# The step widths loaded as a small tile ahead of the weight stream, and the first norm's root, sums and splits in another order

## The chip, the cores and the metric

The kernel runs on one core of one Trainium2 chip. The metric is the device time of one execution in microseconds (us), from three runs. A core has five engines that run side by side and meet through semaphores: TensorE (PE, matrix products; PEld is its weight load), VectorE (DVE), ScalarE (ACT), GpSimd (POOL) and SyncE (SP), which here only issues DMAs.

## The reference

Two transformer-like layers over a sequence of 256 tokens of width 1024, all in float32. What matters here is how the first one begins:

```python
h = rmsnorm(x, mix_pre_norm[l])        # x * rsqrt(mean(x*x) + 1e-6) * w
u = h @ w_in[l]
u_z, u_xbc, u_dt, u_ly, u_lx, u_g = jnp.split(u, list(IN_SPLITS), axis=-1)
...
dt = jax.nn.softplus(u_dt + dt_bias)   # u_dt: 16 columns, one for each head of the SSD mixer
xbc = jax.nn.silu(causal_dwconv(u_xbc, conv_w, conv_b))
```

`u_dt` are the step widths: 16 of the input projection's columns. The rest of the kernel (two mixers, gates, a feed-forward part, then a second layer with four branches) is the same in both versions.

## The kernel before, in words

Activations lie with features on the 128 partitions and tokens along the free axis: `X` is 8 tiles of 128x256. Every weight passes through one **stream**: `stream_list` names its chunks in order, most of them 256 output columns, that is two **units** of 128x1024 floats (512 KB). The stream has 260 units. SP fetches unit q into one of `NR` = 5 buffers `RAW` (`t_raw`), and for q of 5 and more it waits until unit q-5 has been split. Splitting keeps float32 accuracy with three fast products: ACT copies the unit to a rounded high part `WH` (`split` on ACT, L1232), DVE subtracts to get the low part `WL` (`split` on DVE, L1739; its event is `lo(q)`), both in one of `NS` = 4 buffers, and PE does `three` for each of 8 tiles k (L605, L606, L607): wh by xh, wh by xl, wl by xh. A unit is so 24 matmuls of 128x256.

Each engine's program is written out in one order. The class `Walk` keeps it in step: `walk.unit(ahead)` takes the next unit q and first issues the splits up to q+ahead (3 unless told otherwise), `walk.cols(name)` does so for each unit of a chunk with a `tick` behind each, and a tick lets the lanes (generators with the side work) go on if their time has come. So what an engine does between two splits delays the later one.

The start goes like this. The chunk `dt` is the first of the stream, one unit (q=0): its 128 columns hold the 16 step widths, and the rest of its product is not used. `xbc4`, `xbc5` follow (q=1 to 4), then `g0` (q=5, 6), `xbc0` (7, 8), `g1` (9, 10), `xbc1` (11, 12). `dt`, `xbc4` and `xbc5` are computed from x times the norm's weight (`YBh`, `YBl` in `t_br`) without the root, and scaled by the token's factor afterwards (`ROWR`), since the norm is not known yet. Beside that ACT squares x into `SC0` (8 tiles), DVE adds some of the squares (`square_adds`), PE sums over partitions by products with a column of ones (`norm_sums_first`, `norm_sums_last`, `column_sums`), DVE makes the reciprocal root for 2 columns with an integer guess and three Newton steps (`rsqrt`, `newton`), and PE spreads it over the partitions (`norm_spread`). `h_parts` on DVE (L1754 into `t_arena`, L1744 into `t_hl`), ACT (L1237 into `t_hh`) and POOL (L2448, the odd tiles of `t_hl`) then make the normed input `Hh`, `Hl`, which `g0` is the first chunk to use; `chunk_by_k` there takes both units tile by tile. `norm_spread` stands behind `xbc4` on PE; `h_parts` stands behind all of `xbc5` on DVE and ACT.

Behind `g0`, DVE scales `xbc4` by `ROWR` (L1744, 128x512) and does the convolution's six taps (`xbc_taps`, L1754), for which ACT first evacuates `g0` (`gates(0)`, a tanh; it waits for `hb`, three small operations of DVE, too) and does `conv_first`. Between and behind these come the splits, and the softplus of the step widths.

## Time and profile before

| | |
|---|---|
| median of 3 runs | 880.71 us (880.54 to 880.88) |
| the profiled execution | 881.82 us, its span 880.0 us |
| mean granted clock of TensorE | 0.995 |
| busy share | PE 98%, PEld 89%, DVE 71%, ACT 58%, POOL 8% |
| read from memory | 147.18 MB, 168 GB/s over the span |

The span runs from the first to the last instruction; the profiled execution's own time is 1.82 us longer than its span and 1.11 us above the median. Busy shares are means over stages with different limits.

### The profile page before, as it was taken

The numbers are of one execution on the slowest core, as the hardware profiler recorded it, in microseconds if no ns is written. First come the engines' busy times: TensorE is split into PE (matmuls) and PEld (weight loads), VectorE is DVE, ScalarE is ACT, GpSimd is POOL, SyncE is SP. The second block draws the span as 40 slices with busy tenths as digits, with TensorE's granted clock in tenths as the row PEclk, the third lists the DMA queues.
The fourth block names the chain that finished last, engine by engine and source line by source line (L and its number), as shares of the span: only waits on it lengthen the run. The fifth ranks groups of instructions, "written<-read, shape, count | busy, mean of one in ns | idle before, by whom it ended". The sixth has DMA issues, their size and how long they took to land.

```text
span 880.0 us, 14646 instructions
## 1 busy us (share of the span) xinstructions
PE 859.8 (98%) x5816; PEld 780.8 (89%) x5816; DVE 623.1 (71%) x1124; ACT 509.1 (58%) x826; POOL 73.6 (8%) x76
## 2 busy tenths in 40 slices
PE   6999999999999999999999999999999999999997
PEld 6999999999989999999998799999999776778885
DVE  6787987988867766666656787787456455775765
ACT  5565777665377656656657688544444434454443
POOL 0200002001020211111113000500000000000000
PEclk9999999999999999999999999999999999999999
DMA  9457443457455655555564555643322322365541
GB/s 344 146 194 276 159 145 108 169 179 291 140 186 174 239 190 175 187 191 175 185 198 137 181 188 201 222 145 124 117 97 96 113 104 96 119 205 195 197 146 48
DMA packets 40588, 149.21 MB, mean 170 GB/s; under 512 B 4524, under 2 KB 4680, under 8 KB 39880
## 3 DMA queue, kind: packets, MB, share of 16 engines
q1 hardware_dynamic: 40520, 148.27, 49.3%
q8 instruction: 46, 0.75, 0.3%
q14 instruction: 22, 0.18, 0.1%
HBM read 147.18 MB, written 1.08 MB: 168 GB/s over the span
## 4 chain that ended last, share of the span: by engine, by line
PE 89%; DVE 5%; ACT 3%; issue 1%; DMA 1%; SPq 0%; DVEq 0%; ACTq 0%
PE bank L610 40%; PE bank L605 16%; PE bank L606 16%; PE bank L607 16%; PE bank L613 2%; DVE t_wl L1739 2%; DVE t_arena L1744 1%; DVE t_arena L1754 1%; DVE t_x L1754 1%; ACT t_hh L1237 1%; DMA t_x<-in_xin 1%; DVE t_sm L1751 1%; ACT t_arena L1237 1%; ACT t_wh L1232 0%; ACT t_br L1237 0%
## 5 line engine op out<-in xcount | busy, mean ns | idle before, releaser
L1739 DVE TENSOR_TENSOR t_wl<-t_raw,t_wh 128x1024 fp32r<-128x1024 f32 x260 | 316.5, 1226 | 114.3 <-ACT t_wh L1232 113.4
L1232 ACT ACTIVATE t_wh<-t_raw 128x1024 fp32r<-128x1024 f32 x260 | 273.4, 1058 | 129.1 <-PE bank L610 60.3
L605 PE MATMUL bank<-t_hh,t_wh 128*128 128x256 f32 x1144 | 330.3, 289 | 2.2 <-DVE t_hl L1744 1.5
L607 PE MATMUL bank<-t_hh,t_wl 128*128 128x256 f32 x1144 | 323.6, 283 | 0.0
L606 PE MATMUL bank<-t_hl,t_wh 128*128 128x256 f32 x1144 | 323.5, 283 | 0.0
L605 PEld LDWEIGHTS bank<-t_hh,t_wh 128*128 128x128 f32 x1144 | 219.1, 192 | 6.1 <-issue 4.2
L606 PEld LDWEIGHTS bank<-t_hl,t_wh 128*128 128x128 f32 x1144 | 219.2, 192 | 0.8
L607 PEld LDWEIGHTS bank<-t_hh,t_wl 128*128 128x128 f32 x1144 | 219.1, 192 | 0.0
L610 PE MATMUL bank<-t_wh,t_br 128*128 128x512 f32 x384 | 123.8, 393 | 0.2 <-POOL t_br L2448 0.2
L1754 DVE SCALAR_TENSOR_TENSOR t_arena<-bank,t_par,t_arena 128x255 f32<-128x255 f32 (+2 forms) x184 | 75.3, 474 | 45.0 <-ACT t_arena L1237 44.7
L610 PE MATMUL bank<-t_wh,t_hh 128*128 128x512 f32 x224 | 92.0, 411 | 1.8 <-DVE t_wl L1739 1.8
L610 PE MATMUL bank<-t_wh,t_hl 128*128 128x512 f32 x224 | 88.3, 394 | 0.0
L610 PE MATMUL bank<-t_wl,t_hh 128*128 128x512 f32 x224 | 88.0, 393 | 0.0
L610 PEld LDWEIGHTS bank<-t_wh,t_br 128*128 128x128 f32 x384 | 72.1, 188 | 16.5 <-issue 1.9
L1237 ACT ACTIVATE t_arena<-bank 128x512 f32<-128x512 f32 (+4 forms) x75 | 42.6, 582 | 69.5 <-PE bank L610 57.8
L610 PE MATMUL bank<-t_wl,t_br 128*128 128x512 f32 x192 | 74.9, 390 | 0.0
L2448 POOL TENSOR_TENSOR t_br<-t_arena,t_br 128x256 fp32r<-128x256 f32 x30 | 34.5, 1153 | 437.4 <-ACT t_br L1237 437.4
L610 PE MATMUL bank<-t_arena 128*128 128x128 f32 (+6 forms) x432 | 66.7, 297 | 0.8 <-DVE t_arena L1744 0.8
L610 PEld LDWEIGHTS bank<-t_arena 128*128 128x128 f32 (+3 forms) x432 | 52.0, 176 | 12.7 <-issue 8.2
L1237 ACT ACTIVATE t_arena<-bank,t_par 128x256 f32<-128x256 f32 x76 | 37.6, 546 | 39.3 <-PE bank L607 39.3
L610 PEld LDWEIGHTS bank<-t_wh,t_hh 128*128 128x128 f32 x224 | 42.4, 189 | 12.8 <-DVE t_wl L1739 3.2
L610 PEld LDWEIGHTS bank<-t_wh,t_hl 128*128 128x128 f32 x224 | 42.3, 189 | 9.4
(152 smaller groups left out, 840.3 us busy)
## 6 DMA issues: line engine op xcount, KB each, us to landing
t_raw<-in_ws SPq DMA_DIRECT2D x260, 512.0 KB, 3.9
t_br<-decay SPq DMA_DIRECT2D x1, 2048.0 KB, 8.3
t_arena<-in_post SPq DMA_DIRECT2D x3, 512.0 KB, 5.5
t_arena<-gates SPq DMA_DIRECT2D x1, 1536.0 KB, 10.5
t_x<-in_xin SPq DMA_DIRECT2D x4, 256.0 KB, 5.5
t_bd<-in_bd SPq DMA_DIRECT2D x1, 1024.0 KB, 11.7
t_x<-in_xtok SPq DMA_DIRECT2D x1, 1024.0 KB, 5.8
t_arena<-in_mem SPq DMA_DIRECT2D x1, 1024.0 KB, 8.0
```

The source lines that it names most:

```text
L605: e.matmul(o, wh, xh, start=first, stop=False, skip_group_check=True)
L606: e.matmul(o, wh, xl, start=False, stop=False, skip_group_check=True)
L607: return e.matmul(o, wl, xh, start=False, stop=last, skip_group_check=True)
L610: return e.matmul(o, l, r, start=st, stop=sp, skip_group_check=True)
L613: return e.transpose(o, i, ident[0:i.shape[0], 0:i.shape[0]])
L1232: e.activation(WH[q % NS][:, :], RAW[q % NR][:, :], ACT.Copy, bias=0.0, scale=1.0).then_inc(*hi.now(q))
L1237: return e.activation(o, i, f, bias=bias, scale=scale)
L1739: e.tensor_tensor(WL[q % NS][:, :], RAW[q % NR][:, :], WH[q % NS][:, :].bitcast(F), SUB).then_inc(*lo.now(q))
L1744: return e.tensor_tensor(o, a, b, op)
L1751: return e.tensor_scalar(o, a, s1, s2, op0, op1)
L1754: return e.scalar_tensor_tensor(out=o, in0=a, scalar=s, in1=b, op0=op0, op1=op1)
L2448: return e.tensor_tensor(o, a, b, op)
```

## The change

- The chunk `dt` leaves the stream, which has 259 units then. The 16 columns of step widths and the norm's weight come as one tile of 128x136, `first`, by the first DMA. ACT and DVE split the 16 columns into `DTS` (high part beside low part, 32 columns), and PE multiplies with 32 and 16 stationary columns: 16 matmuls. Where the two parts meet is a product with `fold`, in place of a transposition.
- The DMA order becomes `first`, the four pieces of x, unit 0, the constants, unit 1, the parameters, and the rest of the units.
- ACT and DVE make `YBh`, `YBl` before they split unit 0.
- PE does five float32 products of a tile of zeros into bank 3 first. Nothing reads them.
- The squares are added up by DVE to one tile (two additions more), the column sums over it stand between the two units of `xbc4`, the root is ACT's square root, a reciprocal on DVE and one Newton step. ACT loads the table of the square root at its start.
- `h_parts` on DVE and ACT moves ahead of the splits of later units: on DVE only the units up to 4 are split before it. `g0` is done by units (`chunk_by_units`).

The diff, cut to its core (a line of "..." stands for lines left out):

```diff
     s = []
-    s.append(("dt", "w_in", rng(DTC, 128)))
...
 CON = [("ident", 128), ("ones", 128), ("strict", 128),
-       ("b16", 128), ("b32", 128), ("b64", 128)]
+       ("b16", 128), ("b32", 128), ("b64", 128), ("fold", 16)]
...
 def bank_table():
-    bank, n = {}, 0
+    bank, n = {}, 1
...
         DTR = ar(84, 4, T)
+        DTW = ar(86, 136)
+        DTX, WMIX = DTW[:, 0:128].rearrange("p (k c) -> p k c", k=8), DTW[:, 128:136]
+        DTS = WH[NS - 1][:, 0:256].rearrange("p (k c) -> p k c", k=8)
...
         cols_dt = SM[:, 96:160].rearrange("p (a b) -> p a b", a=4)
-        dtr, acs = DTR[0:16, 0, :], DTR[0:16, 1, :]
+        dtr, acs = DTR[0:32, 0, :], DTR[0:16, 1, :]
...
                 e.dma_start(RAW[q % NR][:, :], ws[c, :, 1024 * u:1024 * u + 1024]).then_inc(s_raw[q % NR], 16)
-            fetch(0)
-            e.dma_start(parT[:, :], par).then_inc(s_par, 16)
+            e.dma_start(DTW, first).then_inc(s_first, 16)
             for i in range(4):
                 e.dma_start(X[:, 2 * i:2 * i + 2, :], xin[:, 2 * i:2 * i + 2, :]).then_inc(s_x[i], 16)
+            fetch(0)
             e.dma_start(conT[:, :], con).then_inc(s_con, 16)
-            for q in range(1, NR):
+            fetch(1)
+            e.dma_start(parT[:, :], par).then_inc(s_par, 16)
+            for q in range(2, NR):
...
                     e.dma_start(POSTW["fpost"], post[1]).then_inc(s_post["fpost"], 16)
-                if q == 24:
+                if q == 23:
                     e.wait_ge(*d_dt.of("acs"))
                     e.dma_start(decay, acs).then_inc(s_decay[0], 16)
-                if q == 27:
+                if q == 26:
...
                     walk.tick()
+            def chunk_by_units(name, xh, xl, x_ready):
+
+                b = BANK[name]
+                for j in range(2):
+                    q = walk.unit(NS - 1 - j)
+                    wh, wl = weights(q, 8)
+                    split_ready(q)
+                    if j == 0:
+                        bank_free(name)
+                    for k in range(8):
+                        if j == 0:
+                            x_ready(k)
+                        m = three(half(b, j), wh[:, k, :], wl[:, k, :], xh[:, k, :], xl[:, k, :], k == 0, k == 7)
+                    m.then_inc(*unit.now(q))
...
                 return m
+            def mix_sums():
+                e.wait_ge(s_con, 16)
+                e.wait_ge(*d_add.of("mix", 3))
+                column_sums(7, 0, [SC0[:, 0, :]], True, True).then_inc(*p_norm.now("mix", "sum"))
...
                 for hf in range(2):
-                    m = tr(PB[6][:, 16 * hf:16 * hf + 16], dtr[:, 128 * hf:128 * hf + 128])
+                    m = mm(PB[6][:, 16 * hf:16 * hf + 16], dtr[:, 128 * hf:128 * hf + 128], cn("fold", 16)[0:32, :])
...
             walk.lanes = [ssd_lane(), lru_lane(), rows_lane(), dn_lane(), gm_xm_lane(), sw_lane()]
-            chunk_by_k("dt", YBh, YBl, x_weighted)
-            e.wait_ge(s_con, 16)
-            norm_sums_first("mix", 7, SC0)
-            norm_sums_last("mix", 7, SC0)
-            chunk("xbc4", YBh, YBl)
+            e.wait_ge(*d_const.of("warm"))
+            for _ in range(5):
+                mm(PB[3][:, 0:T], SC1[:, 0, 0:128], SC1[:, 0, :])
+            e.wait_ge(*d_dt.of("w"))
+            for k in range(8):
+                e.wait_ge(*d_xw.of(k))
+                mm(PB[6][0:32, 0:T], DTS[:, k, :], YBh[:, k, :], k == 0, False)
+                m = mm(PB[6][0:16, 0:T], DTS[:, k, 0:16], YBl[:, k, :], False, k == 7)
+            m.then_inc(*p_dt.now("dt"))
+            chunk("xbc4", YBh, YBl, {(1, 0): mix_sums})
...
-                    chunk_by_k("g0", Hh, Hl, normed("mix"))
-                    e.wait_ge(*d_f.of("mix", 7))
+                    chunk_by_units("g0", Hh, Hl, normed("mix"))
+                    e.wait_ge(*d_const.of("row"))
...
                 yield from walk.until(2)
-                chunk_done("dt")
-                act(dtr, half(BANK["dt"], 0)[0:16, :], ACT.Copy).then_inc(*a_dt.now("raw"))
+                e.wait_ge(*p_dt.of("dt"))
+                act(dtr, PB[6][0:32, 0:T], ACT.Copy).then_inc(*a_dt.now("raw"))
...
             walk.lanes = [conv_lane(), ssd_lane(), lru_lane(), rows_lane(), dn_lane(), gm_xm_lane(), sw_lane()]
-            split(0)
-            walk.split_to = 1
-            e.wait_ge(s_par, 16)
+            e.wait_ge(*d_const.of("one"))
+            act(SM[:, 392:393], SM[:, 392:393], ACT.Sqrt)
+            e.wait_ge(s_first, 16)
+            act(DTS[:, :, 0:16], DTX, ACT.Copy).then_inc(*a_dt.now("w"))
...
-                act(YBh[:, k, :], X[:, k, :], ACT.Copy, scale=pc("mixpre", k)).then_inc(*a_xw.now(k))
+                act(YBh[:, k, :], X[:, k, :], ACT.Copy, scale=WMIX[:, k:k + 1]).then_inc(*a_xw.now(k))
+            split(0)
             for i in range(4):
                 act(SC0[:, 2 * i:2 * i + 2, :], X[:, 2 * i:2 * i + 2, :], ACT.Square).then_inc(*a_sq.now("mix", i))
-            walk.cols("dt", True)
-            walk.cols("xbc4")
-            walk.cols("xbc5")
+            split(1)
+            walk.split_to = 2
+            walk.unit(2)
+            e.wait_ge(*d_rs.of("mix", "v"))
+            act(NW[:, 2, 0:2], NW[:, 1, 0:2], ACT.Sqrt).then_inc(*a_sq.now("mix", "root"))
+            walk.tick()
+            e.wait_ge(*p_dt.of("dt"))
+            walk.unit(2)
+            walk.tick()
+            e.wait_ge(s_par, 16)
+            walk.unit()
+            walk.tick()
             h_parts("mix", SC1)
+            walk.unit()
+            walk.tick()
...
                     if k < 8:
-                        stt(f[:, k, :], x[:, k, :], pc(w, k), PB[bank][:, 0:T], MUL, MUL).then_inc(*d_f.now(tag, k))
+                        stt(f[:, k, :], x[:, k, :], w[:, k:k + 1], PB[bank][:, 0:T], MUL, MUL).then_inc(*d_f.now(tag, k))
...
             walk.lanes = [ffn_lane(), ssd_lane(), lru_lane(), rows_lane(), dn_lane(), gm_xm_lane(), sw_lane(), dn_out_lane()]
-            split(0)
-            walk.split_to = 1
+            e.memset(SM[:, 392:393], 1.0).then_inc(*d_const.now("one"))
+            e.memset(SC1[:, 0, :], 0.0).then_inc(*d_const.now("warm"))
+            e.wait_ge(*a_dt.of("w"))
+            tt(DTS[:, :, 16:32], DTX, DTS[:, :, 0:16].bitcast(F), SUB).then_inc(*d_dt.now("w"))
             for k in range(8):
                 e.wait_ge(*a_xw.of(k))
-                stt(YBl[:, k, :], X[:, k, :], pc("mixpre", k), YBh[:, k, :].bitcast(F), MUL, SUB).then_inc(*d_xw.now(k))
+                stt(YBl[:, k, :], X[:, k, :], WMIX[:, k:k + 1], YBh[:, k, :].bitcast(F), MUL, SUB).then_inc(*d_xw.now(k))
+            split(0)
             square_adds("mix", SC0)
-            walk.cols("dt", True)
-            rsqrt("mix", NW, 7, 2, 1024, p_norm.of("mix", "sum"))
-            walk.cols("xbc4")
-            e.wait_ge(*p_norm.of("mix", "row"))
+            e.wait_ge(*a_sq.of("mix", 3))
+            e.wait_ge(*d_add.of("mix", 1))
+            tt(SC0[:, 0:2, :], SC0[:, 0:2, :], SC0[:, 6:8, :], ADD).then_inc(*d_add.now("mix", 2))
+            e.wait_ge(*d_add.of("mix", 2))
+            tt(SC0[:, 0, :], SC0[:, 0, :], SC0[:, 1, :], ADD).then_inc(*d_add.now("mix", 3))
+            split(1)
+            walk.split_to = 2
+            o, v, r, t, h = NW[:, 0, 0:2], NW[:, 1, 0:2], NW[:, 2, 0:2], NW[:, 2, 2:4], NW[:, 1, 2:4]
+            e.wait_ge(*p_norm.of("mix", "sum"))
+            ts(v, PB[7][:, 0:2], 1.0 / 1024, MUL, EPS, ADD).then_inc(*d_rs.now("mix", "v"))
+            e.wait_ge(*d_rs.of("mix", "v"))
+            ts(h, v, -0.5, MUL).then_inc(*d_rs.now("mix", "half"))
+            walk.unit(2)
+            e.wait_ge(*a_sq.of("mix", "root"))
+            e.reciprocal(o, r).then_inc(*d_rs.now("mix", "guess"))
+            e.wait_ge(*d_rs.last())
+            tt(t, o, o, MUL).then_inc(*d_rs.now("mix", "oo"))
+            e.wait_ge(*d_rs.last())
+            tt(t, t, h, MUL).then_inc(*d_rs.now("mix", "t"))
+            e.wait_ge(*d_rs.last())
+            stt(o, t, 1.5, o, ADD, MUL).then_inc(*d_rs.now("mix"))
+            walk.tick()
+            walk.unit(2)
+            walk.tick()
+            walk.unit(2)
+            walk.tick()
+            h_parts("mix", SC1, X, WMIX, 7)
             e.tensor_copy(ROWR, PB[7][:, 0:T]).then_inc(*d_const.now("row"))
-            walk.cols("xbc5")
-            h_parts("mix", SC1, X, "mixpre", 7)
+            e.wait_ge(s_par, 16)
+            walk.unit()
+            walk.tick()
...
             walk.lanes = [ffn_lane(), lru_lane(), dn_lane()]
-            walk.cols("dt", True)
...
     con, masks = constants()
+    dt = i["w_in"][0][:, DTC:DTC + 16].reshape(8, P, 16).transpose(1, 0, 2).reshape(P, 128)
     return {
+        "first": np.concatenate([dt, cols["mixpre"]], 1),
```

What the two versions issue on ACT at the start, up to the evacuation of `g0` (L1232 is `split`, L1237 all other activations). Before:

```order
L1232 ACT_TABLE_LOAD
L1232 ACTIVATE t_wh<-t_raw 128x1024
L1237 ACTIVATE t_br<-t_x,t_par 128x256 x8
L1237 ACTIVATE t_arena<-t_x 128x512 x4
L1232 ACTIVATE t_wh<-t_raw 128x1024 x5
L1237 ACTIVATE t_arena<-bank 16x256
L1232 ACTIVATE t_wh<-t_raw 128x1024 x2
L1237 ACTIVATE t_hh<-t_arena 128x256 x8
L1232 ACTIVATE t_wh<-t_raw 128x1024
L1237 ACTIVATE t_arena<-bank,t_sm 128x256 x2
```

Of the change (L1260 is `split`, L1265 the others):

```order
L1265 ACTIVATE t_br<-t_x,t_arena 128x256 x8
L1260 ACTIVATE t_wh<-t_raw 128x1024
L1265 ACTIVATE t_arena<-t_x 128x512 x4
L1260 ACTIVATE t_wh<-t_raw 128x1024 x2
L1265 ACTIVATE t_sm<-t_sm 128x2
L1260 ACTIVATE t_wh<-t_raw 128x1024
L1265 ACTIVATE t_arena<-bank 32x256
L1260 ACTIVATE t_wh<-t_raw 128x1024 x2
L1265 ACTIVATE t_hh<-t_arena 128x256 x8
L1260 ACTIVATE t_wh<-t_raw 128x1024 x2
L1265 ACT_TABLE_LOAD
L1265 ACTIVATE t_arena<-bank,t_sm 128x256 x2
```

Eight splits (units 0 to 7) stood ahead of the normed input, now six (0 to 5); a table load now stands ahead of the evacuation of `g0`, and it waits for the event `hb` of DVE.

On DVE, from the column sums' reading to the first taps. Before (L1739 is `split`; `t_incl`, `t_sm<-bank` and what is around them belong to the step widths; the three TENSOR_SCALAR from `t_par` are `hb`):

```order
L1739 TENSOR_TENSOR t_wl<-t_raw,t_wh 128x1024 x2
L2278 COPY t_arena<-bank 128x256
L1739 TENSOR_TENSOR t_wl<-t_raw,t_wh 128x1024 x2
L1744 TENSOR_TENSOR t_incl<-t_con 128x128
L1754 SCALAR_TENSOR_TENSOR t_sm<-bank,t_sm,t_par 128x16 x2
L1750 TENSOR_SCALAR t_sm<-t_sm 128x32
L1744 TENSOR_TENSOR t_sm<-t_sm 128x32
L1754 SCALAR_TENSOR_TENSOR t_arena<-t_x,t_par,bank 128x256 x2
L1744 TENSOR_TENSOR t_hl<-t_arena,t_hh 128x256
```

Of the change (L1780 is `split`):

```order
L1780 TENSOR_TENSOR t_wl<-t_raw,t_wh 128x1024 x2
L1795 SCALAR_TENSOR_TENSOR t_arena<-t_x,t_arena,bank 128x256 x2
L1785 TENSOR_TENSOR t_hl<-t_arena,t_hh 128x256
...
L2345 COPY t_arena<-bank 128x256
L1780 TENSOR_TENSOR t_wl<-t_raw,t_wh 128x1024 x2
L1785 TENSOR_TENSOR t_incl<-t_con 128x128
L1795 SCALAR_TENSOR_TENSOR t_sm<-bank,t_sm,t_par 128x16 x2
L1791 TENSOR_SCALAR t_sm<-t_sm 128x32
L1785 TENSOR_TENSOR t_sm<-t_sm 128x32
L1791 TENSOR_SCALAR t_sm<-t_par 128x8 x2
L1791 TENSOR_SCALAR t_sm<-t_par 128x16
L1780 TENSOR_TENSOR t_wl<-t_raw,t_wh 128x1024
```

The copy of the row, two splits and the small operations of the step widths stood before the normed input, and stand behind it now. From the last row of either on, the sequence is the same: one split, then the scaling of `xbc4` and its taps.

## Rows read from the trace of the kernel before

**Rows 1.** Waits of PE, whole span: us in total, times, longest.

```profile
PE bank L605 <- DVE t_br L1754: 8.1, 1, 8.1
PE bank L610 <- DVE t_wl L1739: 1.8, 1, 1.8
PE bank L605 <- DVE t_hl L1744: 1.5, 1, 1.5
```

**Rows 2.** Timeline of PE: start, duration, line, count.

```profile
12.85 1.92 PE L610 MATMUL bank<-t_con,t_arena 128*128 128x1 f32 x16 [0.18 <-DVE t_arena L1744]
...
28.45 0.28 PE L607 MATMUL bank<-t_br,t_wl 128*128 128x256 f32 x1
30.23 0.35 PE L605 MATMUL bank<-t_hh,t_wh 128*128 128x256 f32 x1 [1.50 <-DVE t_hl L1744]
...
52.52 0.39 PE L605 MATMUL bank<-t_hh,t_wh 128*128 128x256 f32 x1 [0.36 <-DVE t_wl L1739]
```

**Rows 3.** Timeline of DVE.

```profile
13.28 3.50 DVE L1739 TENSOR_TENSOR t_wl<-t_raw,t_wh 128x1024 fp32r<-128x1024 f32 x3 [0.57 <-ACT t_wh L1232]
...
16.69 0.15 DVE L1751 TENSOR_SCALAR t_sm<-bank 128x2 f32<-128x2 f32 x1
...
22.61 0.42 DVE L2278 COPY t_arena<-bank 128x256 f32<-128x256 f32 x1 [0.41 <-PE bank L610]
...
26.64 1.23 DVE L1739 TENSOR_TENSOR t_wl<-t_raw,t_wh 128x1024 fp32r<-128x1024 f32 x1 [2.09 <-ACT t_wh L1232]
...
28.71 0.87 DVE L1754 SCALAR_TENSOR_TENSOR t_arena<-t_x,t_par,bank 128x256 f32<-128x256 f32 x2
...
33.57 0.42 DVE L1744 TENSOR_TENSOR t_hl<-t_arena,t_hh 128x256 fp32r<-128x256 f32 x1
...
36.20 0.68 DVE L1744 TENSOR_TENSOR t_arena<-bank,t_arena 128x512 f32<-128x512 f32 x1
38.11 2.45 DVE L1754 SCALAR_TENSOR_TENSOR t_arena<-t_arena,t_par 128x255 f32<-128x255 f32 x6 [1.23 <-ACT t_arena L1237]
```

**Rows 4.** Timeline of ACT.

```profile
4.91 1.06 ACT L1232 ACTIVATE t_wh<-t_raw 128x1024 fp32r<-128x1024 f32 x1 [2.90 <-DMA t_raw<-in_ws]
...
10.12 2.18 ACT L1237 ACTIVATE t_arena<-t_x 128x512 f32<-128x512 f32 x4
...
19.88 1.06 ACT L1232 ACTIVATE t_wh<-t_raw 128x1024 fp32r<-128x1024 f32 x1 [3.37 <-DMA t_raw<-in_ws]
...
29.22 0.81 ACT L1237 ACTIVATE t_hh<-t_arena 128x256 fp32r<-128x256 f32 x2 [2.61 <-DVE t_arena L1754]
...
36.25 0.84 ACT L1237 ACTIVATE t_arena<-bank,t_sm 128x256 f32<-128x256 f32 x2 [1.38 <-PE bank L607]
...
41.15 1.28 ACT L1237 ACT_TABLE_LOAD   x1
42.45 0.63 ACT L1237 ACTIVATE t_arena<-t_arena 128x512 f32<-128x512 f32 x1
```

**Rows 5.** DMA issues on SP's queue, timeline.

```profile
0.72 0.38 SPq L549 DMA_DIRECT2D t_raw<-in_ws  x1
...
1.63 1.85 SPq L554 DMA_DIRECT2D t_x<-in_xin  x4
```

**Rows 6.** Instructions on the tile X, 0 to 25 us: its activations, its landings.

```profile
L1237 ACT ACTIVATE t_br<-t_x,t_par x8: 492/493/508, 6.9 to 9.7; 128x256 fp32r<-128x256 f32 x8
...
DMA to landing us min/median/max: 5.2/5.5/5.8
```

**Rows 7.** By stretch: from:to, length, busy (count) PE PEld DVE ACT POOL, PEclk, DMA share, GB/s.

```profile
14.60:18.20 3.60, 3.60 (x19) 3.60 (x19) 3.46 (x11) 1.68 (x2) 0.00 (x0) 0.53 1.02 424
...
60.00:80.00 20.00, 20.00 (x166) 19.89 (x166) 13.17 (x25) 10.91 (x16) 0.00 (x0) 1.00 0.79 278
```

**Rows 8.** The same view, around the longest wait inside the span.

```profile
485.86:489.29 3.43, 1.59 (x7) 1.01 (x6) 3.32 (x10) 2.09 (x6) 0.00 (x0) 1.00 0.16 48
489.29:492.70 3.41, 3.41 (x11) 2.56 (x10) 2.97 (x8) 3.41 (x5) 0.00 (x0) 0.50 0.36 133
```

More of the change, by code:

```diff
@@ L327, in dn_bank, with build_program @@
     return 3 + (DN_AT[name] + 1) % 3
-def build_program(nc, ws, par, con, masks, bd, rows, swt, xin, xtok, min_, post, decay, gates2, out):
+def build_program(nc, first, ws, par, con, masks, bd, rows, swt, xin, xtok, min_, post, decay, gates2, out):
     ctx = ExitStack()
```

8 lines of the change are left out of this document (4 added, 4 removed).

## The prediction, made before the changed kernel had been run

> **What bounds the kernel now.** The waits of PE over the whole span come first: the longest is the start (8.1 us), then 1.8 us in the middle and 1.5 us for the normed input [rows 1]. In the stretch from 60 to 80 us PE is busy for 20.00 of 20.00 us, with 166 matmuls, so 0.12 us each [rows 7]. PE is therefore the bound from about 52 us on, and what the start does to the end is a shift: by as much as PE reaches the second unit of `xbc1` (at 52.52 now) earlier, the end comes earlier. The work that the change touches lies wholly ahead of that point.
>
> Next the timelines of the start. PE starts at 8.1, does `dt`, then sums over the squares (12.85 for 1.92 us, 16 rows, 0.12 each), then `xbc4` and `xbc5`, whose last matmul begins at 28.45. It then waits for the normed input until 30.23 and later for a split until 52.52 [rows 2]. The reader is to see who ends those two waits: DVE both times. And between them DVE hardly rests: the normed input ends at 33.57 + 0.42 = 33.99, the scaling of `xbc4` starts at 36.20 and its taps at 38.11, after ACT has evacuated `g0` and done the first tap (36.25 to 38.11) [rows 3, 4]. From these taps on, DVE's and ACT's sequence is the same in both versions, up to the split that PE waits for at 52.52. So I follow one event: **the start of the first taps, 38.11 now**. Where PE itself is no later, the end moves as this event moves.
>
> **What the change removes from PE.** The unit `dt`, 24 matmuls (2.9 us at 0.12), for 16; and 12 of the 16 rows of column sums, 1.4 us at 0.12. The stall at 8.1 us is cut too. PE's own saving is thus above 5 us (worked out below), but it isn't what is handed on: DVE is.
>
> **The chain of the new start, step by step.**
> 1. *Unit 0 lands at 8.4.* It is now the sixth DMA, behind 70 KB, four pieces of x of 256 KB each, and itself 512 KB: some 1.6 MB. The sixth one now is the last piece of x, issued at 3.05 or so and landed 5.8 later, 8.85, with 1.8 MB through; the one before it, with 0.25 MB less, some 0.65 earlier [rows 5, 6]. I take 8.4. Bounds: 8.2 to 8.9. The eight scalings of x (3.3 us on ACT, 6.9 to 9.7 plus 0.5 [rows 6]) start when the first piece has landed; as second DMA that is not before the 4.9 at which ACT starts on the first one now less the difference in size, so 4.2 to 4.9, and end by 7.5 to 8.2, under cover of unit 0.
> 2. *`xbc4` begins at 10.7.* ACT's split takes 1.06, DVE's 1.23, begun 1.08 after the former [rows 4, 3]: 8.4 + 2.3. Now its weight matmuls begin at about 14.6, behind the column sums (12.85 + 1.92 [rows 2]).
> 3. *The column sums are done between 14.9 and 15.8.* They wait for PE's unit, for DVE's four additions and for the split of unit 1. ACT: 9.5, squares 2.1 to 11.5 [rows 4], split to 12.6. DVE: additions from 10.7 on, three at 0.7 and one at 0.4, to 13.2; split at 1.14 a piece [rows 3] (three in 3.50) to 14.4. PE's first unit: 24 at 0.12 = 2.9, done by 13.6; or at the low clock, at which 19 took 3.60 (0.19 each, granted 0.53) [rows 7], 4.6, done by 15.3. Then 4 rows of sums, 0.5.
> 4. *The root is done between 17.3 and 18.3.* Two small operations (0.15 each and about 0.2 from start to start, as at 16.69 [rows 3]), 0.4; the split of unit 2, 1.14; a reciprocal and three small ones, 0.9. The square root of ACT lies beside the split. What stood here before, 16 small operations, was hidden under PE, and its saving alone is worth nothing.
> 5. *DVE is ready for the normed input between 19.6 and 20.6*, behind the splits of units 3 and 4 (2.28).
> 6. *ACT is ready for it at 21.15.* Ahead of it stands the split of unit 5, and this unit's DMA is the limit: now ACT idles 3.37 us for it and starts at 19.88 [rows 4]. At 424 GB/s the DMA engines are full at that time [rows 7]; 78 KB more lie ahead of it (`first`, `fold`), 0.2 us. So 20.1, plus 1.05. That its fetch now waits for the split of unit 0 at 10.7 costs nothing: the masks and the block-diagonal weights (1.3 MB, 3 us) are queued in front of it and what is before them is through at 15.6 only.
> 7. *The normed input ends at 25.9.* From the first part on ACT to the last on DVE it is 29.22 to 33.99 = 4.77 now [rows 4, 3], and the loop is the same.
> 8. *DVE's event `hb` at 30.4.* Copy 0.35 (0.42 less overlap); one split at 1.14; then one split with the small work of the step widths, 26.64 to 28.71 = 2.07; then the three operations of `hb`, 36.20 - 33.99 = 2.2 less the split in it (1.3), 0.9 [rows 3]. 25.9 + 4.5.
> 9. *The taps at 33.6.* ACT's table load is new here and waits for `hb`: 1.30 from its start to the next activation (41.15 to 42.45). Then from `g0`'s evacuation to the taps 1.86, as 36.25 to 38.11 [rows 4, 3]. DVE's split and scaling (1.3 + 0.7) lie beside it.
>
> 38.11 - 33.6 = **4.5 us**.
>
> **Is PE there in time?** Sums at 14.9 to 15.8, the rest of the unit 2.9, spreading 0.5, `xbc5` 5.8, `fold` 0.25: `g0` starts at 24.3 to 25.2. Its first unit meets the normed input, whose last tile (on POOL) is there at 26.6, and ends at 27.2 to 28.1; the second needs DVE's split at 27.4, and ends at 30.1 to 31.0; `xbc0` ends at 35.9 to 36.8. The next unit's split is the one behind the taps, 3.6 after their start: 37.2. So PE waits a little there (0.4 to 1.3) and the 1.5 us wait of before [rows 1] moves to this place in a smaller form. The next wait, now at 52.52, is then at 48.0. PE's own shift would be 5 to 5.8 us, which is the upper end if DVE lags less.
>
> **The ends of the costs that before doesn't show.** The five products of zeros run while PE would idle (0.7 to about 5.5, ahead of the first scaled x). A float32 product shows as two rows (8 products of the column sums are the 16 rows of [rows 2]). If each took five times a weight matmul at the low clock (0.19), some 1 us, the five would end by 6.2, ahead of 10.7: nothing lost. At best they bring the high clock to the first unit, 1.7 us on PE, all of it under step 6: nothing won. The 32 and 16 columns wide products can't take more than full ones (0.21 at the low clock), 3.4 us for 16, paced by ACT anyway. The small DMA of 544-byte lines: 0.1 to 1 us later than I assume moves step 1, but steps 1 to 5 have 0.5 to 1.5 us of slack against step 6.
>
> Of the table load the trace shows 1.28, with the next activation 1.30 after its start and ACT without idle time ahead of it [rows 4]. The Trainium skill (ScalarE: Activation LUTs, What ACT_TABLE_LOAD costs) gives 1.28 us for the load and a drain of 1.38 besides, 2.66 a switch; by that the saving would be 3.1 in place of 4.5. The trace has the load alone, and I go by it.
>
> **The sum.** 880.7 - 4.5 = **876.2 us**. In terms of the profiled execution: 881.8 - 4.5 = 877.3, with a span of 875.5. Its own time is 1.1 above the median, and I take that distance as the same.
>
> **The rivals.**
> - *More than that* (chance 0.22). In the middle, PE waits 1.8 us, is busy for 1.59 of 3.43 us, and then has a stretch of 3.41 us with granted clock 0.50 [rows 1, 8]. If the clock stayed high there, PE would end its 11 rows of that stretch in half the time, 1.7 us, of which DVE's splits behind it leave some 1.1. The change moves this place in time; whether the clock falls again I can't tell. With it, or with PE's own shift at the start (5.3 to 5.8), the time is 875.1, at most 874.2. Against it: the three runs agree within 0.34 us, so it doesn't come and go by itself. The Trainium skill (TensorE: Matmul & The Clock Gate, Part 1) says the clock is judged at moments that do not restart with the kernel; by that the place would differ from run to run, which those three runs do not show.
> - *Less* (0.10). A pause of ACT ahead of the table load, or the first unit at the low clock with unit 0 landing at 8.9 and more, each 0.5 to 1.4 us. For the pause: ACT's evacuation of `g0` hangs directly on it. Against: step 9's row. 880.7 - 3.1 = 877.6, down to 878.9.
> - *No change that can be told* (0.04). DVE and ACT could hand nothing on if what bounds 30 to 52 us were PE. Against: both waits of rows 2 end with DVE. 880.
> - *Slower* (0.04). All rests on x coming first. `first` is waited for by ACT ahead of everything, and the scalings of x ahead of the split of unit 0, so each us that `first`, x or unit 0 is late beyond the slack of steps 1 to 5 is a us of the end. From unit 0 at 8.4 + 1 (slack) + 4.5 = 13.9 on nothing is won, and with 15.7 the kernel takes 882.5. For it: 128 short lines and then 2 KB lines ahead of the 4 KB ones. Against: x lands 5.2 to 5.8 us after its issue now, with 0.75 MB ahead of it [rows 6].
>
> **How the numbers follow.** The likeliest case has 0.60, with 875.4 to 877.1: the slack of steps 3 to 6 used up or not. What a measurement here can tell from no change is 0.2%, 1.8 us, so faster means below 878.9. Faster: 0.60 + 0.22 + 0.09; same: 0.05; slower: 0.04. The range that leaves out 2 in 10 reaches into both neighbours: 874.4 to 877.9.
>
> **What would show it.** `xbc4`'s first matmul at 10.7; ACT waiting for unit 5's DMA until 20.1; the normed input's first part on ACT at 21.1; a table load of 1.28 that starts behind `hb` at 30.4; the taps at 33.6; a short wait of PE for a split at 37.2 and one that ends at 48.0. Wrong would be: a first split of unit 0 after 10, a clock of 0.5 that returns more than once, ACT idle ahead of the table load, or PE waiting in 60 to 200 us, where it has next to no wait now.

## The result and the profile after

| | before | with the change |
|---|---|---|
| median of 9 runs | 880.77 us (880.29 to 882.50) | 878.13 us (877.65 to 879.50) |
| the profiled execution, its span | 881.82, 880.0 | 877.81, 876.0 |
| ratio of the times, 95% interval | | 0.9971 (0.9961 to 0.9981) |

The change makes the kernel 2.6 us faster (1.7 to 3.4), where 4.5 were forecast. The same kernel in a second series gave 877.74 against 881.15, 3.4 us. The head of the page of the profile with the change:

```profile
span 876.0 us, 14627 instructions
PE 859.8 (98%) x5808; PEld 778.0 (89%) x5808; DVE 621.7 (71%) x1118; ACT 509.8 (58%) x829; POOL 75.9 (9%) x76
```

ACT's timeline of the start with the change (start, duration, engine, line, operation, out<-in, count, and in brackets the idle time before it and what ended it). L1260 is its split:

```profile
5.54 3.31 ACT L1265 ACTIVATE t_br<-t_x,t_arena 128x256 fp32r<-128x256 f32 x8 [2.69 <-DMA t_x<-in_xin]
9.73 1.06 ACT L1260 ACTIVATE t_wh<-t_raw 128x1024 fp32r<-128x1024 f32 x1 [0.88 <-DMA t_raw<-in_ws]
...
16.65 0.20 ACT L1265 ACTIVATE t_sm<-t_sm 128x2 f32<-128x2 f32 x1 [1.65 <-DVE t_sm L1792]
...
20.94 1.06 ACT L1260 ACTIVATE t_wh<-t_raw 128x1024 fp32r<-128x1024 f32 x1 [1.92 <-DMA t_raw<-in_ws]
21.91 0.71 ACT L1265 ACTIVATE t_hh<-t_arena 128x256 fp32r<-128x256 f32 x2
...
31.66 1.28 ACT L1265 ACT_TABLE_LOAD   x1 [3.15 <-DVE t_sm L1791]
32.95 0.84 ACT L1265 ACTIVATE t_arena<-bank,t_sm 128x256 f32<-128x256 f32 x2
```

This answers to [rows 4]. ACT waits for x (5.54), for unit 0 (9.73), for the column sums (16.65) and for unit 5 (20.94), and then begins the normed input at once. So unit 5's DMA ends the last wait ahead of the normed input, as forecast, 0.8 us later than forecast. The table load waits for `hb`, and the evacuation of `g0` begins 1.29 after the load.

DVE's timeline of the same stretch (L1780 is its split, L1795 from `t_x` the normed input's first half, L1785 into `t_hl` its second):

```profile
11.96 2.67 DVE L1785 TENSOR_TENSOR t_arena<-t_arena 128x512 f32<-128x512 f32 x4
...
16.46 0.16 DVE L1792 TENSOR_SCALAR t_sm<-bank 128x2 f32<-128x2 f32 x1 [0.70 <-PE bank L616]
...
18.53 2.35 DVE L1780 TENSOR_TENSOR t_wl<-t_raw,t_wh 128x1024 fp32r<-128x1024 f32 x2
20.80 0.86 DVE L1795 SCALAR_TENSOR_TENSOR t_arena<-t_x,t_arena,bank 128x256 f32<-128x256 f32 x2
...
26.24 0.43 DVE L1785 TENSOR_TENSOR t_hl<-t_arena,t_hh 128x256 fp32r<-128x256 f32 x1
...
26.92 3.03 DVE L1780 TENSOR_TENSOR t_wl<-t_raw,t_wh 128x1024 fp32r<-128x1024 f32 x2
...
31.00 0.58 DVE L1791 TENSOR_SCALAR t_sm<-t_par 128x8 f32<-128x8 f32 x3
...
34.80 2.45 DVE L1795 SCALAR_TENSOR_TENSOR t_arena<-t_arena,t_par 128x255 f32<-128x255 f32 x6 [1.49 <-ACT t_arena L1265]
```

The taps begin at 34.80, where it was 38.11 [rows 3]: 3.31 earlier. The same form of two splits takes 2.35 at 18.53 and 3.03 at 26.92. What POOL does in that second stretch, from its timeline:

```profile
27.37 1.50 POOL L2575 CAST t_maskW<-t_arena 128x384 bf16<-128x384 f32 x1
28.82 1.28 POOL L2576 COPY t_maskD<-t_arena 128x128 f32<-128x128 f32 x1
```

Last PE, four of the rows of its timeline where it waited:

```profile
6.71 3.59 PE L616 MATMUL bank<-t_br,t_wh 128*32 128x256 f32 x16 [0.88 <-DVE t_br L1795]
12.10 0.39 PE L611 MATMUL bank<-t_br,t_wh 128*128 128x256 f32 x1 [1.80 <-DVE t_wl L1780]
...
38.44 0.39 PE L611 MATMUL bank<-t_hh,t_wh 128*128 128x256 f32 x1 [0.60 <-DVE t_wl L1780]
...
49.20 0.39 PE L611 MATMUL bank<-t_hh,t_wh 128*128 128x256 f32 x1 [0.36 <-DVE t_wl L1780]
```

The wait of 1.50 for the normed input [rows 2] is gone. The wait that ended at 52.52 ends at 49.20, 3.32 earlier: the end has moved by what the taps have. Another 0.8 comes from the middle. The stretches there that answer to [rows 8] (busy time of PE, PEld, DVE, ACT, POOL with their instructions; granted clock, DMA share, GB/s):

```profile
482.50:485.90 3.40, 1.76 (x8) 1.12 (x8) 3.29 (x11) 2.22 (x6) 0.00 (x0) 1.00 0.11 20
485.90:489.30 3.40, 2.63 (x17) 2.02 (x16) 2.96 (x7) 3.40 (x5) 0.00 (x0) 1.00 0.44 146
```

In this execution the granted clock is 1.00 there, the upper of its two levels (2.4 GHz), and not 0.50. ACT's same instruction lies 3.32 earlier with the change ahead of this place (468.43 for 471.75) and 4.17 earlier behind it (502.30 for 506.47), so the place gives 0.85 in this pair of traces (1.1 were estimated); 0.2 of it is lost again by the end, and the spans differ by 4.0. The medians show only 2.6: the execution profiled before lay 1.1 above its median and the one with the change 0.3 below.

### The profile page after: what moved, and what is told of

It reads as the page before. It is cut to its first block, busy times and chain, and to the rows that moved or that the text cites. A ratio compares the mean times of both kernels' runs of the same rounds, so it can differ in the third digit from the quotient of the medians.

```text
span 876.0 us, 14627 instructions
## 1 busy us (share of the span) xinstructions
PE 859.8 (98%) x5808; PEld 778.0 (89%) x5808; DVE 621.7 (71%) x1118; ACT 509.8 (58%) x829; POOL 75.9 (9%) x76
## 4 chain that ended last, share of the span: by engine, by line
PE 87%; DVE 6%; ACT 3%; DMA 2%; issue 1%; SPq 0%; DVEq 0%; ACTq 0%
PE bank L616 40%; PE bank L611 15%; PE bank L613 15%; PE bank L612 15%; PE bank L619 2%; DVE t_wl L1780 2%; DMA t_raw<-in_ws 2%; DVE t_arena L1795 1%; ACT t_hh L1265 1%; DVE t_x L1795 1%; DVE t_arena L1785 1%; DVE t_sm L1792 1%; ACT t_wh L1260 1%; ACT L1265 0%; ACT t_arena L1265 0%
## 5 line engine op out<-in xcount | busy, mean ns | idle before, releaser
L1780 DVE TENSOR_TENSOR t_wl<-t_raw,t_wh 128x1024 fp32r<-128x1024 f32 x259 | 315.6, 1227 | 105.1 <-ACT t_wh L1260 104.3
L1260 ACT ACTIVATE t_wh<-t_raw 128x1024 fp32r<-128x1024 f32 x259 | 272.3, 1058 | 121.1 <-PE bank L616 60.8
L1795 DVE SCALAR_TENSOR_TENSOR t_arena<-bank,t_par,t_arena 128x255 f32<-128x255 f32 (+2 forms) x184 | 75.2, 473 | 45.1 <-ACT t_arena L1265 44.7
L1265 ACT ACTIVATE t_arena<-bank 128x512 f32<-128x512 f32 (+4 forms) x75 | 42.7, 583 | 69.2 <-PE bank L616 57.6
L616 PE MATMUL bank<-t_arena 128*128 128x128 f32 (+6 forms) x442 | 71.3, 305 | 2.0 <-DVE t_arena L2310 1.2
L616 PEld LDWEIGHTS bank<-t_arena 128*128 128x128 f32 (+3 forms) x442 | 55.2, 179 | 14.6 <-issue 8.2
L1265 ACT ACTIVATE t_arena<-bank,t_par 128x256 f32<-128x256 f32 x76 | 37.6, 547 | 39.3 <-PE bank L613 39.3
```

Source lines behind the costliest of these rows:

```text
L616: return e.matmul(o, l, r, start=st, stop=sp, skip_group_check=True)
L1260: e.activation(WH[q % NS][:, :], RAW[q % NR][:, :], ACT.Copy, bias=0.0, scale=1.0).then_inc(*hi.now(q))
L1265: return e.activation(o, i, f, bias=bias, scale=scale)
L1780: e.tensor_tensor(WL[q % NS][:, :], RAW[q % NR][:, :], WH[q % NS][:, :].bitcast(F), SUB).then_inc(*lo.now(q))
L1795: return e.scalar_tensor_tensor(out=o, in0=a, scalar=s, in1=b, op0=op0, op1=op1)
```

## The experiments

My theory: the end moves as DVE's and ACT's chain at the start does, and the gain is short because that chain came later than forecast. The rivals: part of the start's gain is given back further on; and, for the lateness itself, contention with POOL, the DMA order, and the lines in which x is fetched. The letters A and B are each expectation's own (in the first one they are my theory and the first rival); C is POOL, and D the lines of x. Experiments are edits of the changed kernel, unless said otherwise; the difference in time is taken to the change's second series (877.74), and the ratio is always to the kernel before.

**The change once more.** No edit.

> The changed kernel once more, for a second trace. Theory A (the end moves with the start of the first taps, which were at 34.80 us of the span, 38.11 before): taps at 34.8 +- 0.2, PE's wait for a split ends at 49.2 +- 0.2, median 878.1. Theory B (a good part of what is missing to the forecast 4.5 us lies later, in TensorE's clock in the middle, where the first trace had no stretch at 0.50 and before had one of 3.41 us): the taps are where they were, but from 49.2 to the end the distance changes by 0.5 us or more between the two traces.

877.74 us (877.29 to 877.84, 5 runs), ratio 0.9958 (0.9945 to 0.9970). Taps at 34.22, the wait of PE ended at 48.64, span 875.5: against the first trace 0.58 earlier, 0.56 earlier and 0.5 shorter. So A holds for these two traces: behind 49 us they run the same. B falls only as far as they reach, since both executions had the same mean granted clock, 0.999. The 0.6 lies in the DMAs already: unit 0's split began at 9.18, unit 5's at 20.34.

**The normed input back behind the fourth unit.**

```diff
             walk.tick()
-            h_parts("mix", SC1)
             walk.unit()
             walk.tick()
+            h_parts("mix", SC1)
```

(on ACT; on DVE the normed input moves in the same way, and the copy of the row stands ahead of it again)

> The changed kernel with the normed input behind the fourth unit of the first chunks again on DVE and ACT. Theory A: the work of DVE ahead of the event hb is only swapped, so hb stays at 31.5, but g0's first unit is paced by the normed input, whose last tile comes at 31.4 (27.4 now), g0 ends at 34.6 (31.8 now), ACT's evacuation and the taps follow it to 36.5, 1.7 us later, 879.8. Rival (the move is worth nothing, since DVE's total work ahead of the taps is the same): taps at 34.8, 878.1.

881.23 us (880.69 to 882.33), ratio 1.0000 (0.9991 to 1.0008): the whole gain is gone, with the small tile for `dt`, the root on ACT and the single column sum all in place. From ACT's timeline of this kernel, and its stretches:

```profile
26.55 0.81 ACT L1265 ACTIVATE t_hh<-t_arena 128x256 fp32r<-128x256 f32 x2 [2.62 <-DVE t_arena L1795]
...
36.04 0.84 ACT L1265 ACTIVATE t_arena<-bank,t_sm 128x256 f32<-128x256 f32 x2 [2.53 <-PE bank L613]
```

```profile
29.60:33.00 3.40, 3.40 (x16) 3.40 (x17) 3.17 (x8) 2.89 (x5) 2.40 (x4) 0.50 0.01 2
```

The normed input begins at 26.55 in place of 21.91, and the evacuation of `g0` then waits for PE, which had stood idle for 1.19 until 27.57 and ran 16 matmuls in 3.40 us at granted 0.50 behind that. PE's row where that wait ended:

```profile
27.57 0.36 PE L611 MATMUL bank<-t_hh,t_wh 128*128 128x256 f32 x1 [1.19 <-DVE t_hl L1785]
```

The taps come at 37.89. The expectation had 36.5 and 879.8. It had PE end `g0` at 34.6 and ACT's evacuation behind it; the evacuation came at 36.04, and what it had left out is this stretch at the low clock: at the 0.12 of the high clock (an estimate) the 16 matmuls take 1.9 us, 1.5 less. None of the 11 executions of this kernel had a mean granted clock above 0.996. So the whole loss is that of the place of the normed input together with the low clock that came with it.

**The kernel before, with only this move** (and `g0` computed unit by unit, as it needs).

```diff
-            walk.cols("xbc4")
-            walk.cols("xbc5")
+            for _ in range(3):
+                walk.unit(2)
+                walk.tick()
             h_parts("mix", SC1)
+            walk.unit()
+            walk.tick()
```

(on ACT; DVE likewise, with the copy of the row behind `h_parts`)

> The kernel before with one part of the change alone: the normed input moved behind the third unit of the first chunks on DVE and ACT, fewer splits ahead of it, and g0 done by units. Theory A (this move carries the gain, since it takes two splits and the step widths' small work from ahead of the normed input): the normed input starts on ACT at 23.1 (29.22 in before), but PE still has dt's 24 matmuls in front and ends g0 at 34.4, so the taps come at 36.4 (38.11 in before, 34.8 in the change), half of the gain, 879.4. Rival B (the small step-width tile and PE's shorter start carry it): no change from before, 881.1.

879.28 us (878.54 to 880.13), ratio 0.9979 (0.9971 to 0.9988): 2.0 us for this move alone. Taps at 36.55. Here too ACT waits for PE ahead of the evacuation:

```profile
34.70 0.84 ACT L1252 ACTIVATE t_arena<-bank,t_sm 128x256 f32<-128x256 f32 x2 [3.85 <-PE bank L607]
```

So the two halves of the change need each other. The move brings the normed input forward until PE bounds; the rest of the change takes work off PE and is worth something only then. That the small `dt` tile is what counts in this rest was argued, not tried: no run has it alone.

**The root by integer guess and three Newton steps again**, all on DVE:

```diff
-            act(NW[:, 2, 0:2], NW[:, 1, 0:2], ACT.Sqrt).then_inc(*a_sq.now("mix", "root"))
...
+            rsqrt("mix", NW, 7, 2, 1024, p_norm.of("mix", "sum"))
```

> The changed kernel with the integer guess and three Newton steps in place of the square root; ACT's extra table load ahead of g0's evacuation goes with it. Theory A: the root takes DVE 2.9 us from 16.5 on in place of 1.0 beside one split, the normed input begins on ACT at 23.3 (21.9 now), taps at 36.0 though the load is gone: 1.2 us slower, 879.3. Rival (the table load of 1.29 us, which is on the path, costs more than the shorter root gives): taps at 34.8 or earlier, 878.1 or less.

879.27 us (878.34 to 880.72), ratio 0.9979 (0.9969 to 0.9989), 1.5 us slower than the change. From ACT's timeline:

```profile
23.30 0.81 ACT L1265 ACTIVATE t_hh<-t_arena 128x256 fp32r<-128x256 f32 x2 [1.73 <-DVE t_arena L1791]
```

With the Newton steps DVE, and no longer unit 5, is the last to be ready. Taps at 35.89, 1.1 to 1.7 later than with the change, although the table load ahead of the evacuation is gone with the square root. The saving of the square root, hidden in the kernel before, counts once the normed input hangs on it.

**Without the products of zeros.**

```diff
-            e.wait_ge(*d_const.of("warm"))
-            for _ in range(5):
-                mm(PB[3][:, 0:T], SC1[:, 0, 0:128], SC1[:, 0, :])
```

> The changed kernel without the five products of zeros. If they are worth something it is through the clock: unit 0 then runs at the low clock (24 matmuls in 5.1 us), the column sums are done at 17.8 in place of 16.4, DVE reaches the normed input at 22.2 in place of 20.8, behind the landing of unit 5 for the first time; taps at 35.5, 0.7 us slower than the change. Rival (all of it is under the wait for unit 5's DMA, as the prediction had it): taps unchanged.

878.06 us (877.73 to 879.45), ratio 0.9965 (0.9952 to 0.9979): no difference in time that can be told. In PE's timeline the first unit's matmuls start 0.21 apart up to 15.8 and 0.12 apart behind it; with the change they start 0.12 apart from the unit's third on:

```profile
13.05 0.41 PE L611 MATMUL bank<-t_br,t_wh 128*128 128x256 f32 x1
13.26 0.41 PE L612 MATMUL bank<-t_br,t_wh 128*128 128x256 f32 x1
...
16.13 0.28 PE L611 MATMUL bank<-t_br,t_wh 128*128 128x256 f32 x1
16.25 0.28 PE L612 MATMUL bank<-t_br,t_wh 128*128 128x256 f32 x1
```

The granted clock of that stretch:

```profile
12.00:13.00 1.00, 0.76 (x3) 0.76 (x4) 0.96 (x3) 1.00 (x3) 0.00 (x0) 1.00 1.03 419
13.00:14.00 1.00, 1.00 (x7) 1.00 (x6) 0.90 (x2) 0.96 (x2) 0.00 (x0) 1.00 1.03 414
```

The sums are read at 17.38 (16.46 with the change) and DVE is ready at 21.71 (20.80); the normed input on ACT begins 0.31 later, at 22.22. Of that, 0.16 are unit 5, whose split begins at 21.10 (20.94) in this execution. The prediction held that the slack behind the first unit hides all of DVE's 0.9. It hides 0.6 to 0.8 of it.

**Unit 0 ahead of x in SP's order**, as in the kernel before:

```diff
             e.dma_start(DTW, first).then_inc(s_first, 16)
+            fetch(0)
             for i in range(4):
...
-            fetch(0)
```

> The changed kernel with unit 0's DMA ahead of the four pieces of x, as it was before, the rest of the order kept. x then lands last at about 8.9, its eight scalings end at 10.2 and ACT splits unit 0 then: xbc4 begins at 12.5 in place of 12.1. Theory A: the 0.4 us lie within the wait for unit 5 (its landing stays at 20.9), taps at 34.8 +- 0.2, no change. Rival (the order of the first DMAs is a main part of the gain): taps 1 us or more later.

879.56 us (878.60 to 880.29), ratio 0.9977 (0.9968 to 0.9986), 1.8 us slower where no change was expected. ACT's and then PE's timeline:

```profile
7.44 0.91 ACT L1265 ACTIVATE t_br<-t_x,t_arena 128x256 fp32r<-128x256 f32 x2 [4.62 <-DMA t_x<-in_xin]
...
22.07 1.06 ACT L1260 ACTIVATE t_wh<-t_raw 128x1024 fp32r<-128x1024 f32 x1 [0.48 <-PE bank L613]
```

```profile
8.62 3.83 PE L616 MATMUL bank<-t_br,t_wh 128*32 128x256 f32 x16 [3.31 <-DVE t_br L1795]
13.36 0.58 PE L611 MATMUL bank<-t_br,t_wh 128*128 128x256 f32 x1 [0.92 <-DVE t_wl L1780]
```

x comes 1.9 later and unit 0's split, whose data had come earlier, stands behind the scalings. PE idles 3.31 until 8.62, the clock is granted at 0.50 from about 8 to 18 us, the sums are read at 19.03, and DVE and PE are late in place of the DMA. So x first is a real part of the gain. The low clock isn't the reason: the three of the 11 executions with a mean of 0.998 took 879.56 to 879.66. The slack of steps 1 to 5 had been put at 0.5 to 1.5 us. From the rows it is 0.6: without the products of zeros the normed input starts 0.51 after DVE is ready (22.22 for 21.71), and with the change DVE is ready at 20.80, by which it would start at 21.31, but waits for unit 5 until 21.91.

**Masks and block-diagonal weights fetched behind unit 6**, so that unit 5 comes earlier:

```diff
-            e.dma_start(MSK, masks).then_inc(s_msk, 16)
-            e.dma_start(bdT[:, :, :], bd).then_inc(s_bd, 16)
...
+                if q == NR + 1:
+                    e.dma_start(MSK, masks).then_inc(s_msk, 16)
+                    e.dma_start(bdT[:, :, :], bd).then_inc(s_bd, 16)
```

> The changed kernel with the DMAs of the masks and the block-diagonal weights (1.3 MB) behind those of units 5 and 6. Theory A (the landing of unit 5, 20.92, is the limit of the normed input): unit 5 lands at about 17.8, ACT splits it when PE has done unit 1 (19.3), the normed input on ACT starts at 21.3 in place of 21.9, limited by DVE then; taps at 34.2, 0.6 us faster, 877.5. Rival (DVE's own work is the limit): no change of the taps.

876.98 us (876.83 to 878.16), ratio 0.9953 (0.9941 to 0.9966). ACT's timeline of this kernel:

```profile
20.07 1.06 ACT L1261 ACTIVATE t_wh<-t_raw 128x1024 fp32r<-128x1024 f32 x1 [0.47 <-PE bank L614]
21.89 0.81 ACT L1266 ACTIVATE t_hh<-t_arena 128x256 fp32r<-128x256 f32 x2 [0.76 <-DVE t_arena L1796]
```

The wait for unit 5 is gone, which shows that its DMA was the limit. In this trace nothing is won by that: from 12 to 16 us the clock was granted at 0.60, the sums were late (17.04), and DVE took over as the limit, with taps at 34.80 again. The median is 0.8 below the change's, with overlapping intervals. Among executions with the same mean granted clock of 0.999 the two don't overlap: three here took 876.83 to 876.98, five of the change (from both its series) 877.29 to 878.13. So the DMA's wait was worth something where no low clock came.

**POOL's mask work ahead of its normed input**, beside other splits:

```diff
             walk.cols("xbc5")
+            e.wait_ge(s_msk, 16)
+            e.wait_ge(s_con, 16)
+            e.tensor_copy(maskW[:, :], MSK[:, 0:384])
...
             h_low("mix", SC1)
```

> The changed kernel with GpSimd's copies of the masks and two sums ahead of its part of the normed input, so that they don't run beside DVE's splits of units 5 and 6, which took 3.02 us for two there and 2.3 elsewhere. Theory C (the two engines hinder each other): those two splits take 2.3 to 2.4, the taps come 0.6 us earlier, 34.2, unless the splits of units 3 and 4 are now slowed and use up their slack of 0.6. Rival: the splits were late for another reason (their operands), and nothing changes.

878.30 us (877.06 to 878.38), ratio 0.9961 (0.9948 to 0.9973). DVE's two splits, and what ACT's table load then does:

```profile
18.53 2.62 DVE L1780 TENSOR_TENSOR t_wl<-t_raw,t_wh 128x1024 fp32r<-128x1024 f32 x2
...
26.75 2.71 DVE L1780 TENSOR_TENSOR t_wl<-t_raw,t_wh 128x1024 fp32r<-128x1024 f32 x2
```

```profile
30.77 1.28 ACT L1265 ACT_TABLE_LOAD   x1 [2.44 <-DVE t_sm L1791]
```

The later pair takes 2.71 in place of 3.03, the earlier one 2.62 in place of 2.35. From the normed input's end to the table load it is 4.28, not 4.99, and the taps come at 33.91. So what step 8 lacked was mostly POOL, though the splits didn't fall to the expected 2.3 to 2.4: they give 0.3 of the 0.7, and the small operations of the step widths and of `hb` the rest. The 0.7 us don't show in the median, which lies within the spread of the change's.

**The table load drawn forward as well**, by a tanh on one column ahead of the wait for `hb`:

```diff
             walk.tick()
+            act(SM[:, 392:393], SM[:, 392:393], ACT.Tanh)
```

> The changed kernel with GpSimd's mask work early (as in early_pool3) and ACT's table load ahead of its wait for the event hb, by a tanh of one column. The load then lies in ACT's idle time. Theory A: the path is then DVE's split and the scaling of xbc4, which ends 0.35 us ahead of ACT's evacuation now: taps at 33.5, 0.35 us before early_pool3 and no more, though the load is 1.3 us long. Rival (the load's whole 1.3 us are on the path): taps at 32.6.

877.84 us (877.33 to 879.17), ratio 0.9964 (0.9952 to 0.9977). The load runs at 28.59 in idle time of ACT, but the evacuation then waits for PE:

```profile
32.97 0.84 ACT L1265 ACTIVATE t_arena<-bank,t_sm 128x256 f32<-128x256 f32 x2 [1.93 <-PE bank L613]
```

From the normed input's start to the taps it is 11.91, 0.3 less than with POOL's move alone (12.18), as expected, and not the load's whole 1.3. But what stands ahead of the evacuation is PE, and not only DVE's split and scaling as the expectation had it.

**x in two DMAs of 4 KB lines**, for the late unit 0:

```diff
-            for i in range(4):
-                e.dma_start(X[:, 2 * i:2 * i + 2, :], xin[:, 2 * i:2 * i + 2, :]).then_inc(s_x[i], 16)
+            for i in range(2):
+                e.dma_start(X[:, 4 * i:4 * i + 4, :], xin[:, 4 * i:4 * i + 4, :]).then_inc(s_x[i], 16)
```

> The changed kernel with x in two DMAs of 4 KB a partition in place of four of 2 KB. Theory D (unit 0 landed at 9.2 to 9.7 and not at 8.4 because the short lines at the start move little: 0.38 MB less were moved by 10 us than in before): x's last piece lands at 6.7 to 7.0 in place of 7.1 to 7.5, unit 0 at 8.5 to 9.0, unit 5 at 20.0 to 20.4, taps 0.4 to 0.8 us earlier, 33.7 to 34.2. Rival (the slow start belongs to the first DMAs whatever their lines, or to the time of an issue): the same landings within 0.2 us, taps at 34.2 to 34.8.

877.75 us (876.65 to 878.05), ratio 0.9957 (0.9944 to 0.9969), the same as the change. The scalings start at 6.20 (5.54), unit 0 lands at 9.4 (2.09 + 7.3; its split begins at 9.43, at 9.73 and 9.18 with the change), and unit 5's split begins at 20.65. D had unit 0 at 8.5 to 9.0 and unit 5 at 20.0 to 20.4, so D falls: the lines of x don't set when unit 0 lands.

**All of it together**: the early table load, POOL's copies early with its sums left behind, the block-diagonal weights behind unit 6; and then x in two DMAs besides.

```diff
-            e.dma_start(bdT[:, :, :], bd).then_inc(s_bd, 16)
...
+                if q == NR + 1:
+                    e.dma_start(bdT[:, :, :], bd).then_inc(s_bd, 16)
...
+            act(SM[:, 392:393], SM[:, 392:393], ACT.Tanh)
...
+            e.tensor_copy(maskW[:, :], MSK[:, 0:384])
```

> The tail kernel with the block-diagonal weights' DMA (1 MB) behind unit 6 and GpSimd's two sums of masks back behind its part of the normed input. Unit 5 lands at 18.4, and DVE is the limit of the normed input: ACT begins it at 21.3 with a high clock in the first unit, 21.9 otherwise; taps at 33.2 to 33.8, 876.6. If PE is the bound by then (its wait at 37.6 was gone in early_pool3), the taps move but the wait near 48 shrinks and the end moves by less than the taps.

> best1 with x in two DMAs. If theory D of x_two holds, all of the start comes 0.5 us earlier and nothing waits for unit 5's DMA: taps at 32.8, 876.1. If it doesn't, as best1.

877.35 us (876.69 to 878.17), ratio 0.9954 (0.9942 to 0.9967), and 877.07 us (876.38 to 877.89), ratio 0.9953 (0.9939 to 0.9966). Neither can be told from the change (0.9958, 0.9945 to 0.9970). The second one's taps come at 33.99, and ACT waits for PE ahead of them:

```profile
31.91 0.84 ACT L1266 ACTIVATE t_arena<-bank,t_sm 128x256 f32<-128x256 f32 x2 [2.25 <-PE bank L614]
```

## Why the prediction was off

Its direction, its mechanism and its bound were right, and its size was not: 2.6 us (3.4 in the second series) in place of 4.5. What failed are two terms of the sum, the landings of the DMAs (steps 1 and 6, 0.8 us of the taps) and step 8 (0.5 us), and the baseline: 38.11 and 881.8 came from one execution with more of the low clock than most, and I took its distance from the median as fixed.

- **The event followed** (the taps' start moves the end): right. Two pairs of numbers show it: 3.31 and 3.32 against before, 0.58 and 0.56 between the two traces of the change. In the first trace of the change and in those of all twelve experiments the span ends 841.2 to 841.6 behind the start of the taps, wherever these lie between 33.91 and 37.89; in the trace before, with the low clock in the middle, it is 841.9. The short wait of PE behind the taps and the one that ends 14.4 after them came as described, at 38.44 and 49.20.
- **Step 1, unit 0 at 8.4**: wrong, the term that started the miss. ACT's split of it began at 9.73 (9.18 in the second trace), beyond the bounds 8.2 to 8.9. I had reckoned with the amounts that the DMAs moved before. The DMA views of the first 10 us, before and then with the change, have 0.38 MB less with the change:

```profile
DMA packets 1145, 2.74 MB, mean 274 GB/s; under 512 B 120, under 2 KB 248, under 8 KB 1145
```

```profile
DMA packets 1083, 2.36 MB, mean 236 GB/s; under 512 B 111, under 2 KB 239, under 8 KB 1083
```

  By 20 us part of this is made up: 6.74 MB before and 6.49 with the change. At the 417 GB/s that the change's DMAs move from 16 to 20 us the 0.25 MB that are left make 0.6 us (an estimate), most of unit 5's 0.8. And the amounts of one execution are no fixed row: the kernel before with only the move, whose DMA order is that of before, had 2.57 MB in the first 10 us and began unit 5's split at 20.27, not 19.88. Why the DMAs start slower with the new order stays open; long lines for x did not mend it.
- **Steps 2 to 5**: each came later by what step 1 did, less its slack. `xbc4` at 12.10 for 10.7, the sums at 16.46 for 14.9 to 15.8, DVE ready at 20.80 for 19.6 to 20.6.
- **Step 6, unit 5 at 20.1**: the right limit, at 20.94 (20.34). The normed input began at 21.91 (21.31) for 21.15. This is 0.8 of the 1.2 us by which the taps were late in the first trace.
- **Step 7, 4.77**: right, 4.76 (21.91 to 26.67).
- **Step 8, 4.5 to `hb`**: wrong, 4.9 to the end of `hb` and 4.99 to the table load. The two splits stood in the sum at 1.14 each, counted from start to start, and took 2.95 so counted (3.03 with their end), 0.7 more; the small work of the step widths took 0.2 more, and the three operations of `hb` 0.3 less. The splits now lie beside POOL's mask work, which before stood beside `hb` and one split, and the run that moved POOL's work away took 0.7 out of this term.
- **Step 9, 3.2**: right, 31.66 to 34.80 is 3.14. The drain behind the load, by which the Trainium skill (ScalarE: Activation LUTs, What ACT_TABLE_LOAD costs) gets to 2.66 us, is not in this trace: the next activation follows 1.29 after the load's start.
- **The products of zeros** at nothing: right in time, as far as can be told; in the trace they are worth 0.2 to 0.3 us of the normed input. **That all rests on x coming first**, said under "slower", held: with unit 0 first 1.8 us are lost. What was wrong there is only my later expectation of that run, which had no change.
- **The distance to the median**: wrong. The execution profiled before lay 1.1 above its median, and I took that over. The rival "more than that" held that the low clock would not come and go by itself, from three runs. It does. In the three later series the kernel before ran 49 times: 34 executions had a mean granted clock of 0.997 (median 881.2 us), six had 0.995, as the profiled one (882.3), and three had 0.999 (880.3). The trace before has two places at the low clock, at the start [rows 7] and in the middle [rows 8]; in the middle all other traces, the kernel before with only the move among them, have 1.00. Of the change's 14 executions with a clock on record five had 0.999, both profiled ones among them (877.8), and nine 0.994 to 0.996 (878.0). So the traces compare an execution of before with two such places with ones of the change that have none. At 0.999 on both sides the change gives 2.5 us, and by the 841.2 to 841.6 above the taps of the kernel before would then begin at about 37.0 (an estimate; no trace shows it), so about 1 us of the 38.11 would be the low clock at the start, beside the 0.3 to 0.7 by which this trace's 841.9 lies above the others. The Trainium skill (TensorE: Matmul & The Clock Gate, Part 1: judged at moments that do not restart with the kernel) had said so, and these differences between executions of one kernel agree with it.
- **The other rivals**: "no change" and "slower" fell. "Less" named unit 0 at 8.9 and more with the first unit at the low clock; the former came, the latter did not in either trace of the change. But it came in seven of the twelve experiments, and nine of the change's 14 executions had a mean of 0.996 or less, so in many of them both may have met. The range of this rival, 877.6 to 878.9, holds the first median.

What stays open, beside the DMAs' start: shifts of 3.3 and 3.9 us of the taps stand against medians of 2.6 and 3.4 us. The clocks above have the right sign and about the right size for it, but only a trace of the kernel before at a mean of 0.997 or 0.999 could show where its taps begin then, and there is none.

## What to carry to other kernels

An instruction that is late by its place in a queue is worth moving only until the next engine bounds, and what makes that one faster counts only with the move: the two halves of this change gave 2.0 and 0.0 us alone, and 2.6 to 3.4 together. Before a row of one trace becomes a baseline, compare the mean granted clock of the profiled execution with those of the others. When the first DMAs of a kernel change in size or order, reckon their landing times with a margin of 1 us and more, since the trace of before shows them for its own order alone. And a move on one engine changes what its operations overlap with: for each one ask what GpSimd does at its new time.
